# Expert pass 0 of a mixture-of-experts kernel: its input columns come from selection products instead of a gather and transposes

## The reference, cut to what matters

```python
h = h + m_lat[2] * y                                   # residual after the mixer
v = modulate(rmsnorm(h, norm_ffn[l]), m_lat[3], m_lat[4])
...
lg = (xt @ w_grp + b_grp)                              # 4 groups
p_g, grp = lax.top_k(softmax(lg), 1)
le = (xt @ w_exp + b_exp).reshape(T, N_GROUPS, EXP_PER_GROUP)   # 32 experts
top_p, top_i = lax.top_k(softmax(le of the group), TOP_K)       # top 2
gate = p_g * top_p / sum(top_p)
...
xb = x_pad[tok]                                        # the rows of one expert
return (silu(xb @ w1[e]) * (xb @ w3[e])) @ w2[e]       # 1024 -> 512 -> 1024
```

## Time and profile before

| | us |
|---|---|
| median of 3 runs | 2499.48 |
| lowest and highest | 2497.59 and 2507.92 |
| span of the profiled execution | 2494.6 |
| its own time beside the span | not among the numbers; the median lies 4.9 above the span |
| PE busy | 2372.1 (95%) |
| DVE busy | 1143.0 (46%) |
| ACT busy | 361.5 (14%) |
| POOL busy | 294.1 (12%) |
| router's end, layer 0: last residual half to first product of pass 0 | 833.2 to 860.3 |
| the same, layer 1 | 1882.4 to 1909.6 |

### The profile page before, as it was taken

The page is one execution under the profiler, slowest core; times in us unless marked ns, Lnnn a source line. Parts: engine busy times, 40 slices in busy tenths (PEclk is TensorE's granted clock), DMA queues, the critical chain, the costliest instruction groups (busy, mean ns, idle before and its releaser), DMA issues. The chain is left out here.

```text
span 2494.6 us, 33367 instructions
## 1 busy us (share of the span) xinstructions
PE 2372.1 (95%) x14149; PEld 1058.1 (42%) x14150; DVE 1143.0 (46%) x2405; ACT 361.5 (14%) x645; POOL 294.1 (12%) x313
## 2 busy tenths in 40 slices
PE   4999999989999999999999899999999999999997
PEld 3545444544555523333233344444555333334433
DVE  1788377767945423322222544434455223322226
ACT  2310233331012200000000240000121000000002
POOL 2000000001000222122220000000002122221200
PEclk9999999999999999999999999999999999999999
DMA  9577100020170599999999611112106999999994
GB/s 307 200 251 275 34 26 26 17 110 34 68 286 34 213 357 402 402 404 413 388 409 410 240 34 51 34 51 85 76 29 254 378 406 402 414 402 414 406 379 202
DMA packets 140530, 581.41 MB, mean 233 GB/s; under 512 B 16756, under 2 KB 41640, under 8 KB 87768
## 3 DMA queue, kind: packets, MB, share of 16 engines
q1 hardware_dynamic: 120648, 534.87, 55.1%
q0 software_dynamic: 19648, 44.09, 4.8%
q10 hardware_dynamic: 80, 0.26, 0.0%
HBM read 550.74 MB, written 44.32 MB: 239 GB/s over the span
## 5 line engine op out<-in xcount | busy, mean ns | idle before, releaser
L1709 PE MATMUL ps<-arena 128*32 128x512 f32 x6144 | 678.9, 595 | 16.8 <-DMA arena<-in_ex_w_dram 16.8
L1709 PEld LDWEIGHTS ps<-arena 128*32 128x32 f32 x6144 | 207.2, 110 | 440.7 <-issue 423.7
L1744 PE MATMUL ps<-arena 128*32 128x512 f32 x3072 | 344.2, 598 | 11.2 <-DMA arena<-in_ex_w_dram 11.1
L1869 PE MATMUL ps<-arena 128*128 128x512 f32 x616 | 264.5, 592 | 0.0
L2497 DVE TENSOR_TENSOR arena<-arena,ps 128x512 f32<-128x512 f32 x48 | 52.3, 1090 | 456.2 <-PE ps L1709 456.2
L1589 PE MATMUL ps<-arena 128*128 128x512 f32 x512 | 229.4, 598 | 1.6 <-DVE arena L2273 1.6
L1744 PEld LDWEIGHTS ps<-arena 128*32 128x32 f32 x3072 | 119.1, 111 | 226.2 <-issue 207.5
L822 POOL DMA_INDIRECT arena<-normed_rows,arena x184 | 185.7, 1009 | 111.6 <-issue 52.5
L2542 DVE TENSOR_TENSOR arena<-ps,gates 128x512 f32<-128x512 f32 x96 | 61.8, 686 | 257.4 <-PE ps L1744 257.4
L1869 PEld LDWEIGHTS ps<-arena 128*128 128x128 f32 x616 | 117.0, 190 | 147.3 <-issue 147.3
L1402 PE MATMUL ps<-arena 128*128 128x512 f32 x384 | 167.3, 593 | 0.7 <-issue 0.7
(11 more groups left out here) (325 smaller groups left out, 2297.0 us busy)
## 6 DMA issues: line engine op xcount, KB each, us to landing
arena<-in_ex_w_dram SPq DMA_DIRECT2D x384, 1024.0 KB, 10.5
arena<-in_mod_w_dram SPq DMA_DIRECT2D x24, 2048.0 KB, 8.7
arena<-expert_rows SPq DMA_DIRECT2D x16, 1024.0 KB, 7.7
arena<-in_od_w_in_dram SPq DMA_DIRECT2D x12, 1024.0 KB, 5.4
arena<-in_x_dram SPq DMA_DIRECT2D x2, 4096.0 KB, 15.4
expert_rows<-gates SPq DMA_DIRECT2D x8, 1024.0 KB, 22.4
normed_rows<-arena POOLq DMA_DIRECT2D x16, 512.0 KB, 2.9
arena<-in_ev_w_in_dram SPq DMA_DIRECT2D x3, 2048.0 KB, 13.1
```

Of the source, the lines that this page charges most:

```text
L1709: ins = nc.tensor.matmul(bank(2 + m)[c:c + n], x[:, j, c:c + n], w_slot(e % 2, m, KC, FE)[:, j], start=j == 0, stop=j == KC - 1)
L1744: ins = nc.tensor.matmul(bank(5 + half)[c:c + n], HT[:, j * P + c:j * P + c + n], w_slot(e % 2, 2, FC, D)[:, j, half * 512:(half + 1) * 51 ...
L1869: ins = nc.tensor.matmul(bank(4 * (g % 2) + b), x[:, j], y[:, j], start=first and j == 0, stop=j == 3, skip_group_check=True)
```

## The change: selection products

For each token tile, VectorE builds a 128x128 matrix SEL[:, i] in which row t has, at slot s, the value rstd of token t if the token sits in slot s of pass 0, and else zero (`select`). TensorE multiplies the residual tile (as the stationary operand, eight blocks of 128 features) with this matrix and sums over the eight tiles in banks 0 and 1 (`selected`). The sum is what the gather and the transposes made: the scaled rows of pass 0 as columns. `selected(0)` to `selected(7)` stand where the spare products stood. `first_x_cols` moves from `experts` into `mix_and_route`, ahead of the table PIECE. The gather of pass 0, the 32 turning products, the semaphore `row_ready`, and SP's wait for the gathered rows go; `tab_ready` now counts two per layer. The turned columns of the last tile are copied inside `place(6)` instead of behind it. Four spare products are left ahead of pass 0 instead of five. Core of the diff:

```diff
+        SEL, SEL_GATE = at(47104, TT, P), at(35200, 2)
...
         def gathered(l, p):
-            return (12 * l + p // 2 + 1) * 64 - (48 * (l + 1) if p % 2 == 0 else 0)
+            return (12 * l + p // 2 + 1) * 64 if p % 2 else (11 * l + p // 2) * 64
...
                 sp.wait_ge(hn_out[1], 16 * (TT // 2) * (l + 1))
-                sp.wait_ge(x_full[0], gathered(l, 0))
                 weights(1, 1)
...
-                pool.wait_ge(row_ready, 2 * l + 1)
-                gather(l, 0)
-                pool.wait_ge(row_ready, 2 * l + 2)
+                pool.wait_ge(tab_ready, 2 * l + 1)
                 for p in range(1, 4):
                     gather(l, p)
...
+                def selected(i):
+
+                    pe.wait_ge(sel_ready, t0 + i + 1)
+                    if i == 0:
+                        pe.wait_ge(h_ready, 2 * TT * l + 14)
+                    for j in range(KC):
+                        ins = nc.tensor.matmul(bank(j // 4)[:, (j % 4) * P:(j % 4 + 1) * P], H[:, i, j::KC], SEL[:, i],
+                                               start=i == 0 and j % 4 == 0, stop=i == TT - 1 and j % 4 == 3,
+                                               skip_group_check=True)
+                    if i == TT - 1:
+                        ins.then_inc(x_T, 1)
...
                 places(TT - 2)
-                pe.wait_ge(h_ready, 2 * TT * (l + 1) - 1)
-                spare(2, 2)
+                selected(0)
                 turn_rows(TT - 1)
-                spare(4, 2)
+                selected(1)
                 logits(TT - 1)
+                for i in range(2, 4):
+                    selected(i)
                 table_of_rows(TT - 2)
-                spare(8, 2)
+                selected(4)
                 places(TT - 1)
                 nc.tensor.matmul(bank(4)[:, 0:NE], ones, RUN[:, TT - 1], start=True, stop=True).then_inc(pos_mm, 1)
-                spare(4, 2)
+                for i in range(5, TT - 1):
+                    selected(i)
                 table_of_rows(TT - 1)
-                spare(3, 2)
+                selected(TT - 1)
                 pe.wait_ge(hot_ready, t0 + l + TT + 1)
...
-                spare(8, 2)
...
-                pe.wait_ge(x_full[0], gathered(l, 0))
-                for j in range(KC):
-                    for g in range(4):
-                        ins = nc.tensor.matmul(
-                            bank(j // 4)[32 * g:32 * g + 32, (j % 4) * P:(j % 4 + 1) * P],
-                            XG[:, 0, g * 256 + j * 32:g * 256 + j * 32 + 32], ident, start=True, stop=True)
-                ins.then_inc(x_T, 1)
                 pe.wait_ge(h_ready, 2 * TT * (l + 1))
-                spare(5, 2)
+                spare(4, 2)
...
+                def select(i):
+
+                    link(V.tensor_scalar(SEL_GATE, SC[:, 8:10, i], float(CAP), rstd[:, i:i + 1], ALU.is_lt, ALU.mult))
+                    link(V.scalar_tensor_tensor(out=SEL_GATE, in0=PASS_OF[:, :, i], scalar=0.0, in1=SEL_GATE,
+                                                op0=ALU.is_equal, op1=ALU.mult))
+                    link(V.tensor_scalar(SEL[:, i], HOT0[:, 0, i], SEL_GATE[:, 0:1], None, ALU.mult))
+                    V.scalar_tensor_tensor(out=SEL[:, i], in0=HOT0[:, 1, i], scalar=SEL_GATE[:, 1:2], in1=SEL[:, i],
+                                           op0=ALU.mult, op1=ALU.add).then_inc(sel_ready, 1)
...
                     residual(i, 1)
+                    if i >= 2:
+                        select(i - 2)
                     if i < TT - 1:
                         mean_square(i)
                         scale(i)
-                place(TT - 2)
-                mean_square(TT - 1)
-                columns_of(TT - 1)
+                place(TT - 2, last_columns)
+                select(TT - 2)
                 scale(TT - 1)
                 route(TT - 1)
...
                 place(TT - 1)
+                select(TT - 1)
                 dve.wait_ge(tab_mm, 2 * l + 1)
                 rows_out(bank(7)[:, 0:NP], PASS_F, PASS_ROW, PASS_TOK)
-                dve.sem_inc(row_ready, 1)
                 V.tensor_copy(TOK_F, PASS_TOK).then_inc(hot_ready, 1)
+                first_x_cols(l)
                 dve.wait_ge(tab_mm, 2 * l + 2)
```

More of the change, by code:

```diff
@@ L382, in build @@
         hot_ready = sem("hot_ready")
+        sel_ready = sem("sel_ready")
         tab_mm = sem("tab_mm")
         placed = sem("placed")
-        row_ready = sem("row_ready")
         tab_ready = sem("tab_ready")
@@ L718, in _ @@
                 sp.wait_ge(y_mm, NP * (l + 1))
-                sp.wait_ge(tab_ready, l + 1)
+                sp.wait_ge(tab_ready, 2 * l + 2)
                 moe_overflow(l)
@@ L812, in gather @@
                 b = p % 2
-                if p >= 2:
+                if p > 2:
                     pool.wait_ge(x_T, l * NP + p - 1)
                     pool.wait_ge(x_full[b], gathered(l, p - 2))
[L816 to L820, removed]
                 for t in range(4):
@@ L862, in overflow @@
             def overflow(l):
-                pool.wait_ge(tab_ready, l + 1)
+                pool.wait_ge(tab_ready, 2 * l + 2)
                 flag = pool.value_load(ANY[0:1, 0:1])
@@ L1222, in _ @@
                 experts(l)
-                act.wait_ge(tab_ready, l + 1)
+                act.wait_ge(tab_ready, 2 * l + 2)
                 overflow(l)
@@ L1764, in experts @@
                     else:
-                        pe.wait_ge(tab_ready, l + 1)
+                        pe.wait_ge(tab_ready, 2 * l + 2)
                     turn_hidden(p)
@@ L2273, in _, with first_x_cols @@
                     V.tensor_tensor(MIX[:, HC + c, sl], tmp, MIX[:, HC + c, sl], ALU.mult).then_inc(hmix_ready, 1)
+            def first_x_cols(l):
+                dve.wait_ge(x_T, l * NP + 1)
+                for j in range(KC // 2):
+                    ins = V.tensor_scalar(XT[:, 0, j * P:(j + 1) * P], bank(0)[:, j * P:(j + 1) * P],
+                                          gain_x[:, 2 * l + 1, j:j + 1], mod[:, l, 3, j:j + 1],
+                                          ALU.mult, ALU.add)
+                ins.then_inc(xt_ready, 1)
             def mix_and_route(l, tmp):
@@ L2351, in route, with place @@
                     dve.sem_inc(oh_ready, 1)
-                def place(i):
+                def place(i, between=None):
                     place_, first, slot = [SC[:, q:q + 2, i] for q in (8, 10, 12)]
@@ L2370, in place @@
                     link(V.tensor_reduce(pass_, OVER, AX.X, ALU.add))
+                    if between:
+                        between()
                     for k in range(2):
@@ L2379, in place, with last_columns @@
                     dve.sem_inc(hot_ready, 1)
+                def select(i):
[5 more added lines that the diff above has]
+                                           op0=ALU.mult, op1=ALU.add).then_inc(sel_ready, 1)
+                def last_columns():
+                    mean_square(TT - 1)
+                    columns_of(TT - 1)
                 for i in range(TT):
@@ L2409, in mix_and_route @@
                 link(V.tensor_copy(PIECE, PIECE_F))
-                dve.sem_inc(row_ready, 1)
+                dve.sem_inc(tab_ready, 1)
                 dve.wait_ge(pos_mm, (l + 1) * (TT + 1))
@@ L2501, in experts @@
                 n0 = l * NP
[L2503 to L2509, removed]
                 def x_cols(p):
@@ L2560, in late_hot @@
                     dve.sem_inc(late_ready, 1)
-                first_x_cols()
                 for p in range(NP):
@@ L2582, in overflow @@
             def overflow(l):
-                dve.wait_ge(tab_ready, l + 1)
+                dve.wait_ge(tab_ready, 2 * l + 2)
                 dve.wait_ge(late_ready, 4 * TT * l + 3 * TT)
```

## The result

The changed kernel takes 2523.47 us (median of 4, 2519.58 to 2526.40) against 2498.53 for the kernel before: a ratio of 1.0094, 95% interval 1.0077 to 1.0110, slower by 19 to 27 us. The forecast was 2487.4, faster by 12, and the range ended at 2496. One of the twelve runs of experiment 4 had a mean granted clock of 0.80 instead of 0.97 to 0.99 and took 2950 us; it is counted in no time and no ratio here.

The account below looks back on a forecast made before the run. PE, busy 95% of the span, was taken to bound the kernel. Starting pass 0 earlier gives 2 x 6.46 = 12.9, less 0.8 for the clock, 12.1 off 2494.6; plus 4.9 for the median, 2487.4 us, range 2482 to 2496.

Parts of the forecast that it names:

- The step that failed: Selection products ahead of pass 0: strided weights cost nothing, since a tile's turning takes 0.114 us per record.
- The term of 14.9 us per layer: Selection products on PE: 0.116 us per record, 1.86 us per `selected`, 14.9 for eight.
- the 6.46 that pass 0 was to gain: Start of pass 0: PE's work after the last projection sums to 21.55 us, so 6.46 earlier in each layer.
- The upper bound: Selection products: load and product don't overlap, 0.113 + 0.12 = 0.23 us per record; as a rival about 2515, chance 0.05.
- PE ends last everywhere in the tail: Between last projection and pass 0: PE comes later than VectorE's results, by 1.5 us at the places.
- VectorE's six `select`s: Projection-paced iterations: 1.1 us of work each falls in 1.22 us of waiting for ScalarE and costs nothing.
- the margin of 0.5: `select(7)` on VectorE: takes 1.0 to 1.2 us, ready at 849.1, wanted by PE at 849.65.
- The gate matrix: Expert 1's load: net about 4.8 us earlier than now, wanted 7 us after pass 0's start, so covered.
- The gather of pass 1: XT[1] ready at worst 869.6, wanted 869.7, 2 to 4 us slack expected; rival 2495.4, 0.24 together with the full queue.
- The clock: Half clock near pass 0: one drop costs PE 1.6 us; half of one, 0.8, was put into the sum.
- Rival 3, the full queue: Experts' stage: full DMA queue gives half the gain back, 2493.4; chance 0.24 together with the late gather of pass 1.
- SP's wait: SP's 7.1 us wait for the gathered rows: without it, expert 1's gate matrix comes net about 4.8 us earlier.

Follow-up runs that it names:

- experiment 4: Changed kernel with the selection matrix stationary and the residual tile moving, collected rows then copied and transposed: 2489.87 us, ratio 0.9965.
- experiment 1: Changed kernel with the stationary residual tile read in blocks of 128 neighbouring elements instead of every eighth: 2487.5 us, ratio 0.9947.
- experiment 2: Changed kernel with selection products of 64 instead of 128 columns, stride kept: 2526.77 us, a single run.
- experiment 5: Kernel before without SP's wait for the gathered rows of pass 0: 2508.66 us, ratio 1.0036.
- experiment 3: Changed kernel with stationary read strides of 1, 2, 4, 4, 8, 3, 3, 8 elements for tiles 0 to 7: 2511.96 us in one run.

## Why the prediction was wrong, point by point

- *The step that failed*: "The turning of a tile reads H with the same stride as weights and takes 0.91 us for 8 records up to the next line, 0.114 each, so the stride costs nothing." That inference carried the price of the contiguous row over to a strided operand. In a transpose the strided read is free (1.04 us for eight at L1595, and 1.04 for eight contiguous ones at L1298 of the kernel before); in a product it costs 0.243 per record. The term of 14.9 us per layer measured 31.0, which is 16.1 more. Less the 6.46 that pass 0 was to gain, and less 0.55 by which the rest of the sum was too long (experiment 1: 21.00 for 21.55), that makes 9.1 us lost per layer; 9.2 was measured.
- *The upper bound was right in size and wrong in cause.* I had kept 0.23 per record as the bound, from load and product one after the other, and given its rival 0.05 with 2515. Experiments 1 and 2 refute that cause: contiguous loads hide, and half the columns save nothing. Its time lay within 9 us of the result all the same, which was luck. The Trainium skill's rule on overlap, cited in the prediction ("TensorE: Matmul & The Clock Gate", section "The mechanism"), isn't borne out by experiment 1, where loads and products of full rows overlap at 0.117 us per record; the same section also has loads pulled ahead that go to a background weight buffer, which the prediction left out.
- *The row that would have told* was in the trace: the modulation's products read `MROW[:, s, j::KC]` as weights, by the same stride of 8, with two columns. The timeline of weight loads, kernel before:

```profile
44.20 3.88 PEld L1245 LDWEIGHTS ps<-arena 128*128 128x128 f32 x16
```

  3.88 us for 16, 0.243 each, the very time of a `selected`. I chose the nearest row by shape; the nearest by address pattern was this one. With it the sum would have been 31.0 + 6.65 = 37.7 us to pass 0, 9.7 more than before, and 2519.
- *Right*: PE ends last everywhere in the tail (experiment 1: 21.00 against 21.55). VectorE's six `select`s cost nothing that shows: the last projection ended at 827.1 to 833.6 us in the seven profiles with them and at 829.4 to 833.4 in the four without. One costs 1.13 us (832.71 to 833.84), of 1.0 to 1.2. In experiment 1 `select(7)` was done at 849.81 and wanted at 850.28, the margin of 0.5. The gate matrix came in time: up to 900 us, in layer 0, PE waits for no DMA after pass 0 has begun, neither in the changed kernel nor in experiment 1.
- *The gather of pass 1*: never late. In the contiguous version it landed at 864.25, 9.1 us after its first issue at 855.20, and XT[1] was ready at 867.9, 2.5 us before PE wanted it: within the 2 to 4 I expected. The changed kernel has the same 2.5 (882.5 and 885.0). That rival fell.
- *The clock*: a drop came in layer 0 (0.55 at 843 to 846) but cost nothing, since the strided records don't slow with the array.
- *Rival 3, the full queue*: not shown. Experiment 1's interval holds the whole gain of 14 us (ratio 0.9944).
- *SP's wait*: I took its removal only as a gate matrix that comes earlier. Experiment 5 shows that the wait had value while the gather stood.

## What to carry to other kernels

Price an added product by the row whose operands are read in the same way, stride included, and not by the row with the same shape; look for the stationary operand's address pattern in the code of every candidate row. When PE ends last in a stretch, a stationary float32 operand read by a stride of three elements or more sets the pace of its products, so make the matrix that you build yourself, contiguous, the stationary one, and stream the other in wide pieces, as experiment 4 did. And before taking out a wait of a DMA queue, ask which transfer it keeps the road clear for.

## What the runs showed of the hardware that I had not expected

- A float32 load of 128x128 weights from SBUF takes 0.117, 0.124, 0.178, 0.236 and 0.243 us per record at element strides 1, 2, 3, 4 and 8 (experiment 3). At stride 8 it doesn't depend on the granted clock, 3.91 us for 16 at 0.50 and 3.88 at 1.00; without a stride it does, 3.51 and 1.88 for the logits' 16 (experiment 2).
- A transpose that reads the same tile by stride 8 runs at 0.11 per record (0.88 us for eight wherever the clock was 1.00, 1.71 at 0.50). Why it escapes the price of the stride was not tried; the rows show only that it does.
- One gather of 128 rows of 4 KB went from 5.6 to 6.4 us between issue and use to 9.25 when 2 MB of weights were queued beside it (experiment 5, both layers).
